# Two transformer blocks with a mixture of experts: the last projection by token tiles, the first expert panels issued place by place, and the two experts of a pair one behind the other

## The reference: what is computed

```python
def hybrid_mixer(...):                      # y_ssd: 1024 features, y_att: 1024 features
    mixed = jnp.concatenate([y_ssd, y_att], axis=-1)
    return mixed @ w_out                    # w_out: 2048 x 1024, float32

h = h + hybrid_mixer(rmsnorm(h, norm_mix), ...)
t = rmsnorm(h, norm_ffn)
group_logits  = t @ w_router_group          # 8 groups
expert_logits = t @ w_router_expert         # 64 experts, 8 in each group
# each token goes to the best two experts of its best group; for each expert e and its tokens xb:
hid = jax.nn.silu(xb @ w_gate[e]) * (xb @ w_up[e])     # 1024 x 512, 1024 x 512
y   = hid @ w_down[e]                                  # 512 x 1024
h = h + sum of gate_weight * y;  out = rmsnorm(h, norm_final)
```

## Time and profile before

| what | us |
|---|---|
| median of 3 runs | 1533.67 (1533.14 to 1534.39) |
| the profiled execution's own time | 1533.78 |
| its span (first to last instruction) | 1531.8 |
| experts: first matmul | 636.5 from the span's start |
| experts: start of the last pair's `down` | 1513.7 |
| mean granted PE clock | 0.988 of 2.4 GHz |

### The profile page before, as it was taken

How to read it: one execution, slowest core, us unless ns; L and a number is a source line. 1 busy time by engine, 2 the same in 40 slices (tenths; PEclk the granted TensorE clock), 3 DMA queues, 4 the chain that set the end, 5 groups by cost and what they waited for, 6 DMA issues and landing times.

```text
span 1531.8 us, 20132 instructions
## 1 busy us (share of the span) xinstructions
PE 1452.1 (95%) x7657; PEld 879.1 (57%) x7657; DVE 565.3 (37%) x869; ACT 455.0 (30%) x773; POOL 69.9 (5%) x62
## 2 busy tenths in 40 slices
PE   7999999999999999999999988988988989999997
PEld 6888988888889877543444333332432433444342
DVE  5865877753677968411111111110110111111112
ACT  5634655533565674311111111110110111111112
POOL 1000000000020082100000000000000000000000
PEclk9999999999999999999999999999999999999999
DMA  9564346454554446999999999999999999999996
GB/s 329 172 219 165 138 159 214 171 205 153 192 165 166 111 138 214 415 420 419 414 423 422 422 422 422 422 421 423 422 422 422 422 421 422 423 421 417 423 421 252
DMA packets 110133, 491.84 MB, mean 321 GB/s; under 512 B 9655, under 2 KB 15931, under 8 KB 63484
## 3 DMA queue, kind: packets, MB, share of 16 engines
q1 hardware_dynamic: 108364, 484.43, 79.8%
q0 software_dynamic: 1504, 6.37, 1.3%
q10 hardware_dynamic: 208, 0.28, 0.1%
HBM read 508.82 MB, written 1.10 MB: 333 GB/s over the span
## 4 chain that ended last, share of the span: by engine, by line
PE 67%; DMA 23%; DVE 4%; POOL 2%; issue 2%; ACT 1%; SPq 1%; DVEq 0%; ACTq 0%; POOLq 0%
DMA slots<-in_w_up_dram 22%; PE banks L1648 20%; PE banks L1124 20%; PE banks L1683 8%; PE banks L1191 7%; PE banks L1192 3%; PE banks L1590 3%; PE banks L1600 2%; POOL areas L615 1%; DVE w_split L1788 1%; POOL areas L614 1%; SPq L497 1%; PE banks L1114 1%; DVE areas L2091 0%; ACT w_split L700 0%
## 5 line engine op out<-in xcount | busy, mean ns | idle before, releaser
L1648 PE MATMUL banks<-slots,xeT 128*64 128x512 f32 x1536 | 353.4, 614 | 40.5 <-DMA slots<-in_w_up_dram 40.5
L1648 PEld LDWEIGHTS banks<-slots,xeT 128*64 128x64 f32 x1536 | 111.8, 141 | 277.0 <-issue 213.8
L1683 PE MATMUL banks<-slots,heT 128*64 128x512 f32 x1024 | 226.8, 595 | 8.0 <-ACT heT L1043 8.0
L1788 DVE TENSOR_TENSOR w_split<-raw,w_split 128x2048 fp32r<-128x2048 f32 (+1 forms) x96 | 206.0, 2171 | 76.5 <-ACT w_split L700 76.4
L700 ACT ACTIVATE w_split<-raw 128x2048 fp32r<-128x2048 f32 (+1 forms) x95 | 168.4, 1806 | 59.5 <-PE banks L1124 54.5
L2367 DVE TENSOR_TENSOR h_e<-banks,h_e 128x512 f32<-128x512 f32 x32 | 22.1, 692 | 420.9 <-PE banks L1648 420.9
L1191 PE MATMUL banks<-h_both,w_split 128*128 128x512 f32 x448 | 158.2, 398 | 0.0
L1683 PEld LDWEIGHTS banks<-slots,heT 128*64 128x64 f32 x1024 | 70.7, 137 | 145.2 <-issue 131.1
L1124 PE MATMUL banks<-w_split,h_both 128*128 128x512 f32 (+1 forms) x624 | 143.1, 385 | 2.4 <-DVE h_both L1778 2.3
L2379 DVE SCALAR_TENSOR_TENSOR y_lo<-banks,stats,y_hi 128x512 fp32r<-128x512 f32 x63 | 44.4, 746 | 230.3 <-ACT y_hi L1057 230.3
L1124 PEld LDWEIGHTS banks<-w_split,h_both 128*128 128x128 f32 x624 | 112.1, 188 | 26.8 <-issue 3.8
(11 more groups left out here) (355 smaller groups left out, 1422.7 us busy)
## 6 DMA issues: line engine op xcount, KB each, us to landing
slots<-in_w_up_dram SPq DMA_DIRECT2D x126, 1024.0 KB
slots<-in_w_down_dram SPq DMA_DIRECT2D x126, 1024.0 KB
areas<-in_w_gate_dram SPq DMA_DIRECT2D x64, 1024.0 KB, 17.7
slots<-in_w_gate_dram SPq DMA_DIRECT2D x64, 1024.0 KB
raw<-in_w_in_dram SPq DMA_DIRECT2D x38, 1024.0 KB, 5.4
raw<-in_w_ff_dram SPq DMA_DIRECT2D x32, 1024.0 KB, 5.3
raw<-in_w_out_dram SPq DMA_DIRECT2D x8, 1024.0 KB, 5.1
raw<-in_w_in_dram SPq DMA_DIRECT2D x10, 512.0 KB, 4.0
```

The costliest lines, as they stand in the source:

```text
L1648: last = mm(bank[SLOTS * e:SLOTS * e + SLOTS, :], xeT[:, k, odd, SLOTS * e:SLOTS * e + SLOTS], expert_panel(w, e, odd)[:, k, :], start=(k ...
L1683: last = mm(banks[half][SLOTS * e:SLOTS * e + SLOTS, :], heT[:, c, SLOTS * e:SLOTS * e + SLOTS], expert_panel("down", e, odd)[:, c, 512 * ...
L1788: last = tt(lo, source, hi, ALU.subtract)
```

## The change

It has three parts, which share no data but the places of the panels.

**1. The last projection by token tiles.** The second half of `project_state(1, ...)` is written out: first the 4 row blocks of token tile 0, then those of tile 1, and the four transposes of tile 0's new `x` stand in the middle of tile 1's products. Router products, transposes, DVE's add and scaling, ACT's scaling and squares, and POOL's `t_made` follow one tile at a time. The squares of `y` go to `area(1)` instead of `xtok`.

```diff
+            sp.wait_ge(xdt_ready, 1)
+            sp.wait_ge(skipped, MT)
+            first_load("gate", 0, 0, 0)
+            sp.wait_ge(turned, turns_before(T_ATT) + 4)
+            sp.wait_ge(mean_ready, ATT_NORM)
+            first_load("gate", 0, 1, 1)
...
-                for piece in range(3 if closing else 2):
-                    half = min(piece, 1)
-                    if not isinstance(i, int) or (w == "gate" and i > 1) or (w != "gate" and i > 0):
-                        sp.wait_ge(used, 2 * i - (3 if w == "gate" else 1) + half)
+                every_row = 4 if w == "down" else 8
+                for e in range(2):
+                    if not isinstance(i, int) or i > 0:
+                        sp.wait_ge(used, 2 * i - (3 if w == "gate" else 1) + e)
+                    at_once = every_row // 2 if closing and e else every_row
+                    for start in range(0, every_row, at_once):
...
             for half in range(2):
-                pool.wait_ge(x_ready, X_OUT1 + 2 * half + 2)
                 for m in range(MT):
+                    pool.wait_ge(x_ready, X_OUT1 + 2 * half + m + 1)
...
-            project_state(1, 1)
+            def turn_rows(m):
+                pe.wait_ge(x_ready, X_OUT1 + 3 + m)
...
+            for m in range(MT):
+                for k in range(4, KT):
+                    if (m, k) == (1, 6):
+                        turn_rows(0)
+                    ins = product(banks[5 + 2 * m][:, :], h, (every, k, slice(P * m, P * m + P)),
+                                  parts(last_panel), (every, k, every), k == 4, k == KT - 1)
+                ins.then_inc(half_projected, 1)
...
-                    for k in range(KT):
-                        if k % 4 == 0 and w == "gate":
-                            pe.wait_ge(pair_landed["odd_gate" if odd else w, k // 4], 32 * (couple + 1))
-                        for e in range(2):
+                    for e in range(2):
+                        if w == "gate":
+                            pe.wait_ge(pair_landed["odd_gate" if odd else w, e], 16 * (couple + 2))
+                        else:
+                            pe.wait_ge(pair_landed[w, e], 16 * (i + 2))
+                        for k in range(KT):
                             last = mm(bank[SLOTS * e:SLOTS * e + SLOTS, :], xeT[:, k, odd, SLOTS * e:SLOTS * e + SLOTS],
                                       expert_panel(w, e, odd)[:, k, :], start=(k == 0), stop=(k == KT - 1))
-                        if k % 4 == 3:
-                            last.then_inc(done, 1)
+                        last.then_inc(done, 1)
...
+                down(0, 0, 0, 1, 2, 3)
+                down(0, 1, 0, 1, 2, 3).then_inc(downed, 1)
...
+                    down(1, 0, 2, 3).then_inc(half_downed, PAIRS // 2)
+                    down(1, 1, 2, 3).then_inc(downed, 1)
```

More of the change, by code:

```diff
@@ L499, in load, with first_load @@
                                      **cond).then_inc(landed_now, 16)
+            def first_load(w, odd, e, half):
+                rows = 2 if w == "down" else 4
+                part = slice(rows * half, rows * half + rows)
+                sp.dma_start(expert_panel(w, e, odd)[:, part, :], {"gate": w_gate, "up": w_up, "down": w_down}[w][0, 2 * odd + e]
+                             .rearrange("(p k) n -> p k n", p=P)[:, part, :]).then_inc(pair_landed["odd_gate" if odd else w, e], 16)
             def tokens_of(pair, e):
@@ L995, in _ @@
                 part = slice(512 * g, 512 * g + 512)
[L996 removed]
+                last = act_(squared[:, 2 * m + g, :], y[:, m, part], ACT.Square, accum_out=stats[:, 2 * m + g:2 * m + g + 1])
             last.then_inc(squares, 1)
@@ L1607, in scatter_whole, with scatter @@
                           start=False, stop=True, skip_group_check=reopened[0])
-            def scatter():
-                for m in range(MT):
+            def scatter(tiles=range(MT)):
+                for m in tiles:
                     for half in range(2):
                         last = scatter_half(half, m)
-                last.then_inc(scattered, 1)
+                if tiles[-1] == MT - 1:
+                    last.then_inc(scattered, 1)
             def last_scatter(final):
@@ L1660, in experts @@
                     scatter()
+                if odd and last_one:
+                    pe.wait_ge(ye_a, 2 * i)
+                    pe.wait_ge(ye_d, i)
+                    scatter((0,))
                 pe.wait_ge(he_ready, i + 1)
@@ L1673, in experts @@
                     gather(couple + 1, 1)
-                if odd and not last_one:
-                    scatter()
+                if odd:
+                    scatter((1,) if last_one else range(MT))
                 pe.wait_ge(heT_ready, i + 1)
@@ L1679, in experts, with down @@
                     pe.wait_ge(xe_d, 2 * couple + 4)
-                pe.wait_ge(pair_landed["down", 0], 32 * (i + 1))
-                def down(c, half):
-                    for e in range(2):
+                def down(e, half, *chunks):
+                    for c in chunks:
                         last = mm(banks[half][SLOTS * e:SLOTS * e + SLOTS, :], heT[:, c, SLOTS * e:SLOTS * e + SLOTS],
```

139 lines of the change are left out of this document (78 added, 61 removed).

## The result

The changed kernel takes 1865.94 us (median; 1864.45 to 1867.53) beside 1533.47 for the kernel before (1533.14 to 1534.39): **1.216 times as long**, 95% interval 1.2143 to 1.2177. The forecast was 1531, with 1520 to 1545 as its range.

What follows compares the result with a forecast made beforehand. DMA was taken to set the pace in the middle (29.8 us per pair), PE in early and late stretches (25.8). Terms +2.4 + 10 - 13.1 + 0 - 2.2 = -2.9 on 1533.78 gave 1531 (rounded), range 1520 to 1545.

Steps and rivals of the forecast that it cites:

- Part 3, matmuls expert by expert: Expert matmuls, all of expert 0 then expert 1: PE looks far enough ahead to run both side by side; 0, bounds 0 to +4.
- a partial reach: Rival at the expert matmuls: PE looks ahead under 16 instructions but not strictly in order; between 1545 and 2137, 6%.
- the strict case: Rival at the expert matmuls: experts run one after the other, 46.5 us per pair, end at 2137; 12%.
- Part 1, the start: Last projection by token tiles, before the experts: first expert matmul at 635.5 instead of 636.48, -1.0 us, bounds 0 and -1.6.
- Part 2: First panels issued earlier: 16 pieces land near 632.5, but DMA then idles until PE gives back a place; 0.
- Part 3, release by expert: Places come back after an expert's 16 steps instead of 8, so a dry DMA restarts 3.4 us later; +2.4 and +10.
- the further dry points: Stretches at PE's pace behind the start, where DMA runs out of orders and restarts later: together +10 us.
- the moved scatter: Last pair: the scatter between gate and up moves into PE's waits for `h_e` and `heT`; -1.4 us.
- the ones near 1300: Two dry points near 1300 and 1320, where a faster DMA runs out of orders: 2.1 us added.
- Part 3, larger packets: Expert loads in rows of 16 KB: 1.5% less time per byte, half of an extrapolated 3.0%; -13.1 us.
- The end: Last pair: moved scatter -1.4, and the first output half of the last `down` read 0.8 earlier; -2.2 us.

Runs made afterwards that it cites:

- part 1 alone: The kernel before with only the last projection, router, squares and `t_made` changed to go by token tiles; 1534.91 us, ratio 0.9999.
- runs of 2: Two of PE's instructions per expert in a row; the 17.9 compares With 8 KB rows (1551.32 us) with the kernel of parts 1 and 2 (1533.41 us).
- With 16 KB rows: The changed kernel with PE's order back to two instructions per expert in a row, loads still one 2 MiB DMA per expert; 1543.20 us, ratio 1.0049.
- With 8 KB rows: As With 16 KB rows, but each expert's matrix loaded by two 1 MiB DMAs in rows of 8 KB; 1551.32 us, ratio 1.0104.
- the kernel of parts 1 and 2: The kernel before with the last projection by token tiles and the first 16 pieces issued place by place, experts unchanged; 1533.41 us, ratio 0.9996.
- the kernel with runs of 2: The changed kernel with only PE's order of expert matmuls undone, rows of 16 KB and release by matrix kept; 1543.20 us, ratio 1.0049.
- runs of 8: Eight of PE's instructions per expert in a row: in the changed kernel 1563.61 us, ratio 1.0186; in the kernel before 1573.41 us, ratio 1.0237.
- runs of 16: Sixteen of PE's instructions per expert in a row: the changed kernel, 1865.94 us, ratio 1.216; this order alone in the kernel before, 1871.87 us, ratio 1.2199.

## Why the prediction was wrong

**The step that failed** is "Part 3, matmuls expert by expert": "I take it that it looks far enough: 0". PE's reach is four instructions, and 16 were needed. (Four counts the one that starts in the same step: in the rows from 709.97 on, `gate`'s first overtakes three of `down`. In the prediction's own counting, by instructions overtaken, one was proven, three is what PE does, and 15 were needed.) The prediction had said that 16 steps for 32 instructions prove an overtaking of one instruction only, and that no row has a longer run; it then put 82% on a reach fifteen times the proven one. In place of its 0 the runs show 12.3 us per pair, and all but 9 of the 332 us gone when this order alone is undone. The price was there, between 1545 and 2137 for a partial reach, with 6%. Nothing in the trace of before spoke for a long reach; the two ends of what rows could bound, 0 and the strict case, should both have weighed. An unknown that is worth 600 us against a sum of -3 decides the forecast, not the sum.

The Trainium skill, "TensorE: Matmul & The Clock Gate", section "The mechanism", has weight loads reordered in a window of 64 and matmuls never. The second does not hold in this trace: the first matmul of `gate` at 709.97 starts ahead of the three of `down` at 710.39, 710.82 and 711.25, which stand before it in the program. And a window of 64 doesn't help matmuls here: the reach of 4 is the whole of it.

**Part 1, the start.** Right in its working: -1.13 us from the first of the 24 products to the experts, -1.0 forecast. Whether it moves the end by as much is not shown: part 1 alone measured 0.9999, and its interval holds both -1.0 and 0. That the DMA loses only 0.7 us there speaks for less.

**Part 2.** Right: the fill ends near 633 (632.5), the DMA rests until 643 (644.5), and nothing comes of it.

**Part 3, release by expert.** Right in kind, too small in size: 13.4 forecast (3.4 at the start and 10 at the further dry points), less the 1.4 of the moved scatter, which the measured kernel has too: 12.0, beside 17.9 measured at runs of 2. With 16 KB rows the dry points were where they were named (the one near 1385 at 1388 to 1392 with 41 GB/s, the one near 1408 at 1412 to 1416 with 66), each costs some 3.5 us, and the ones near 1300 cost more than the 2.1 that were put on them: 94 GB/s in 1268 to 1272 and 254 in 1300 to 1304 are some 5 us. With 8 KB rows there is one dry point more than forecast: 98, 104 and 150 GB/s in 1384 to 1388, 1396 to 1400 and 1420 to 1424, where the kernel of parts 1 and 2 has one of 295.

**Part 3, larger packets.** The rate is as forecast: half of 3% was taken, and 429 GB/s for 422 is 1.6% (forecast 427 to 428). In the time it is some 8 us, not 13.1. The likely reason is that in the dry stretches a faster DMA only waits longer; it was not tested by itself.

**The end.** From the start of the last `down` to the end of the span it is 22.5 us (1840.34 to 1862.8) instead of 18.1 (1513.72 to 1531.8). `down` itself takes 12.29 instead of 7.09, so the rest is 0.8 shorter: the earlier half of the output, as worked out. The 1.4 for the moved scatter were not measured apart.

**The sum without the failed term** would have been, with what was measured: -0.8 (parts 1 and 2) + 17.9 - 8.1 = 9.0 us slower, which is the kernel with runs of 2 (7.5 by its ratio); the forecast's -2.9 lay on the wrong side even there, through the release and the packets, which were some 6 and 5 us off.

## What to carry to other kernels

Where PE's instructions use only some of its columns, alternate between the column groups at every product, or at most in runs of 4 of PE's instructions (two float32 products here); how loads are cut is another matter, and needs no change of PE's order. Where a step of a forecast needs more of the hardware than any row shows, its price belongs into the forecast with the weight of "unknown", not of "unlikely". And a faster DMA is worth its rate only where places are free: give places back in small pieces where PE sets the pace, and use large rows only where the DMA does.

## What the runs showed of the hardware

- In these kernels PE starts an instruction for a free half of its columns if at most four instructions in front of it are still to be started, the one of the same step counted in. It is a count: with 512 elements it is 4 x 0.43 us, with 256 elements 4 x 0.215. By this rule runs of 8 go alone only in the first four and the last four steps of a stretch, 52 steps for 96 instructions; runs of 16 need 76.
- Rows of 16 KB go at 428 to 429 GB/s in steady flow, rows of 8 KB at 422: 1.5% more.
- The granted clock: before, PE waited up to 4.0 us for panels and its mean clock in 820 to 1240 was 0.97; in the changed kernel, which never waits for the DMA, it is 1.00. At 12 us more per pair that was no gain.
